# One level of Strassen in the up projection of an MLP: 256-token matmuls in place of 512

## What is computed

```
h2  = modulate(rms_norm(x, norm2_w), sh2, sc2)          # 512 x 2048
mlp = square(relu(h2 @ w_mlp1)) @ w_mlp2                # 2048 -> 8192 -> 2048
x   = x + g2 * mlp
out = rms_norm(x, final_norm_w)
```

## Time and profile before

| | |
|---|---|
| time, median of 3 runs | 2270.32 us (2270.09 to 2270.79) |
| the profiled execution | 2271.48 us, span 2269.7 us |
| TensorE busy | 2246.0 us |
| VectorE busy | 1581.5 us |
| ScalarE busy | 832.9 us |

### The profile page before, as it was taken

How to read it: one execution, slowest core, us unless ns; L and a number is a source line. 1 busy time by engine, 2 the same in 40 slices (tenths; PEclk the granted TensorE clock), 3 DMA queues, 4 the chain that set the end, 5 groups by cost and what they waited for, 6 DMA issues and landing times.

```text
span 2269.7 us, 27271 instructions
## 1 busy us (share of the span) xinstructions
PE 2246.0 (99%) x10096; PEld 1833.1 (81%) x10096; DVE 1581.5 (70%) x1898; ACT 832.9 (37%) x1106; POOL 119.1 (5%) x113
## 2 busy tenths in 40 slices
PE   8999999999999999999999999999999999999997
PEld 5588888888887888888888888888888888888886
DVE  8989888867666675634444444344789898989857
ACT  4333333344444422423323333333433333333343
POOL 0011111100101000000000000000000000000000
PEclk9999999999999999999999999999999999999999
DMA  9965777622222565434554455574775555555543
GB/s 400 420 247 203 260 258 255 251 86 81 78 79 75 203 260 194 147 113 176 175 197 173 166 199 179 172 281 171 265 275 206 222 203 191 216 222 203 221 163 135
DMA packets 110705, 455.24 MB, mean 201 GB/s; under 512 B 9009, under 2 KB 13617, under 8 KB 97073
## 3 DMA queue, kind: packets, MB, share of 16 engines
q1 hardware_dynamic: 101680, 394.49, 47.6%
q0 software_dynamic: 8672, 59.77, 7.1%
q10 hardware_dynamic: 290, 0.16, 0.0%
HBM read 390.42 MB, written 63.96 MB: 200 GB/s over the span
## 4 chain that ended last, share of the span: by engine, by line
PE 94%; issue 2%; DVE 2%; DMA 2%; ACT 0%; SPq 0%; POOL 0%; POOLq 0%; DVEq 0%; ACTq 0%
PE bank L733 20%; PE bank L734 20%; PE bank L737 20%; PE bank L1059 8%; PE bank L1050 8%; PE bank L1052 7%; PE bank L799 2%; PE bank L944 2%; PE bank L752 1%; DMA prob<-ada 1%; PE bank L1113 1%; PE bank L1115 1%; PE bank L1122 1%; PE bank L910 1%; DMA staged_kept<-staged_piece 0%
## 5 line engine op out<-in xcount | busy, mean ns | idle before, releaser
L733 PE MATMUL bank<-act_hi,w_hi 128*128 128x512 f32 x2016 | 790.3, 392 | 0.0
L734 PE MATMUL bank<-act_lo,w_hi 128*128 128x512 f32 x2016 | 784.9, 389 | 0.0
L737 PE MATMUL bank<-act_hi,w_lo 128*128 128x512 f32 x2016 | 498.1, 389 | 0.0
L1601 DVE TENSOR_TENSOR w_lo<-raw,w_hi 128x1024 fp32r<-128x1024 f32 x265 | 339.3, 1283 | 227.5 <-ACT w_hi L1201 226.0
L733 PEld LDWEIGHTS bank<-act_hi,w_hi 128*128 128x128 f32 x2016 | 378.6, 188 | 80.0 <-ACT w_hi L1201 1.5
L737 PEld LDWEIGHTS bank<-act_hi,w_lo 128*128 128x128 f32 x2016 | 378.4, 188 | 78.9 <-DVE w_lo L1601 0.5
L734 PEld LDWEIGHTS bank<-act_lo,w_hi 128*128 128x128 f32 x2016 | 378.6, 188 | 77.1
L1201 ACT ACTIVATE w_hi<-raw 128x1024 fp32r<-128x1024 f32 x265 | 279.5, 1055 | 284.4 <-PE bank L737 277.8
L2096 DVE TENSOR_TENSOR up_sb<-relu 128x512 f32<-128x512 f32 x64 | 44.1, 692 | 231.9 <-ACT relu L1463 231.9
L1050 PE MATMUL bank<-w_hi,form_sb 128*128 128x512 f32 x392 | 153.2, 391 | 1.8 <-issue 1.8
L1607 DVE CUSTOM_DVE_ANT_0 ada_sb<-ada_sb,silu_c 128x2048 f32<-128x2048 f32 x64 | 154.0, 2419 | 0.6 <-DMA ada_sb<-ada 0.6
(11 more groups left out here) (257 smaller groups left out, 2577.0 us busy)
## 6 DMA issues: line engine op xcount, KB each, us to landing
raw<-weights SPq DMA_DIRECT2D x272, 512.0 KB, 4.0
ada_sb<-ada SPq DMA_DIRECT2D x79, 1024.0 KB, 5.1
staged_kept<-staged POOLq DMA_DIRECT2D x51, 1024.0 KB, 4.7
form_sb<-staged_kept SPq DMA_DIRECT2D x49, 1024.0 KB, 4.8
quarter_b<-weights SPq DMA_DIRECT2D x18, 2048.0 KB, 11.2
quarter_a<-weights SPq DMA_DIRECT2D x17, 2048.0 KB, 7.9
xy<-x_t SPq DMA_DIRECT2D x16, 512.0 KB, 4.8
prob<-ada SPq DMA_DIRECT2D x8, 1024.0 KB, 10.1
```

What stands on the lines that cost most here:

```text
L733: pe.matmul(acc, stationary, hi, start=first, stop=False)
L734: pe.matmul(acc, stationary, lo, start=False, stop=False)
L737: mm = pe.matmul(acc, w_lo[:, w, i * P128:(i + 1) * P128], hi, start=False, stop=last)
L1601: nc.vector.tensor_tensor(w_lo[:, w], raw[:, r], w_hi[:, w].bitcast(F32), ALU.subtract).then_inc(lo_ready, 1)
```

## The change

Groups 1 to 7 of the up projection are computed by one level of Strassen as well. A unit is a pair of tiles: 256 columns of the weights, in four quadrants (two tiles by two halves of the 2048 rows), against h in four quadrants (two halves of the rows by two halves of the tokens). Seven forms of weights (made by VectorE per unit, in place in `raw`) meet seven forms of h (made once and kept in SBUF: quadrants of `act_hi` and `act_lo`, and `made5`, `made6`, `made3`).

- **TensorE:** `up_unit` replaces `up_tile`: seven steps of 24 matmuls, 256 tokens wide, into three half banks (`UP_CHAIN`), two sets of banks in turn. Some steps wait for ScalarE's copies of a bank (`copied`) or VectorE's closings (`closed`).
- **ScalarE:** per unit seven roundings (`up_hi`, four places), three copies of 128x256 out of PSUM (`copy_out`), and relu and square of the four quadrants (`square_out`); up to two staged forms.
- **VectorE:** per unit seven low halves (`up_lo`, two places), four sums of weights (`up_sum`), three closings (`close`) that add a copied chain to a bank into `up_sb`, and the staging work, now with sums made in place in `up_sb`.
- **Staging:** one place instead of two; the order of the forms is 1, 4, 5, 2, 7, 6, 3.
- **The opening:** during the last tiles of group 0 ScalarE fills `h_all` with the shifted h (`fill_h`, 16 of 128x512), VectorE makes four sums of 128x2048 in place (`sum_h`), and ScalarE and VectorE round forms 5, 3, 6, 7 (`h_hi`, `h_lo`). `normed` writes into `h_all` and no longer waits for a place.
- **Group 7** is written to DRAM unrounded (`pieces_kept`, 4 x 512 KB) and rounded in the last folded unit and at the start of its own product (`piece_high`, `piece_low`).
- **SP:** `load_unit` has four loads a unit; the first quarters and forms of the down projection are loaded during the last unit.

The core of the diff (PE, ScalarE, VectorE; the new `load_unit`, `sum_h`, `stage_lo` and the loads around the loops are told above):

```
+            def up_unit(w, q):
+                first = isinstance(w, int)
+                for k, form in enumerate(UP_FORMS):
+                    if k == 0 and first and w < 2:
+                        pe.wait_ge(relu_ready, BLOCKS)
+                    elif k == 0:
+                        pe.wait_ge(relu21, w - 1)
+                        pe.wait_ge(closed, 3 * w - 5)
+                    if k == 1 and not (first and w < 2):
+                        pe.wait_ge(closed, 3 * w - 3)
+                    if k == 2:
+                        pe.wait_ge(copied, 3 * w + 1)
+                    if k == 4:
+                        pe.wait_ge(copied, 3 * w + 3)
+                    if k == 6:
+                        pe.wait_ge(closed, 3 * w + 2)
...
+                    out = bank[3 * (q % 2) + UP_CHAIN[k]][:, 0:TOK // 2]
+                    high, low = up_hi_at(up_place(q, k)), w_lo[:, up_lo_place(q, k)]
+                    pe.wait_ge(hi_ready, UP_BASE + (N_FORMS * w + (k + 1)))
+                    for kk in range(BLOCKS):
+                        h_hi, h_lo = h_block(form, kk)
+                        cols = slice(kk * P128, (kk + 1) * P128)
+                        pe.matmul(out, high[:, cols], h_hi, start=k in UP_OPENS and kk == 0, stop=False, skip_group_check=True)
+                        pe.matmul(out, high[:, cols], h_lo, start=False, stop=False, skip_group_check=True)
+                    pe.wait_ge(lo_ready, UP_BASE + (N_FORMS * w + (k + 1)))
+                    for kk in range(BLOCKS):
...
+            for q in range(PAIRS):
+                up_unit(q, q)
+            with pe.Fori(1, FOLDED) as g:
+                for q in range(PAIRS):
+                    up_unit(4 * g + q, q)
...
+            def up_unit(g, q, par, w):            # ScalarE
+                up_hi(w, q, 0)
+                if q or not isinstance(g, int):
+                    before = (w - 1, (q - 1) % 4, par if q else 1 - par)
+                    square_out(*before, 1)
+                stage_hi(g, 1 - par, STAGES_A[q])
+                up_hi(w, q, 1)
+                if q or not isinstance(g, int):
+                    square_out(*before, 2)
+                    square_out(*before, 3)
+                copy_out(w, q, 0)
+                for k in (2, 3, 4):
+                    up_hi(w, q, k)
+                copy_out(w, q, 1)
+                up_hi(w, q, 5)
+                if q < 3:
+                    stage_hi(g, 1 - par, STAGES_B[q])
+                copy_out(w, q, 2)
+                up_hi(w, q, 6)
+                square_out(w, q, par, 0)
...
+            def up_unit(g, q, par, w):            # VectorE
+                if q or not isinstance(g, int):
+                    close(w - 1, (q - 1) % 4, par if q else 1 - par, 2)
+                up_lo(w, q, 0)
+                up_sum(w, q, 5)
+                stage_lo(g, 1 - par, STAGES_A[q])
+                up_lo(w, q, 1)
+                up_sum(w, q, 6)
+                up_sum(w, q, 7)
+                up_lo(w, q, 2)
+                up_sum(w, q, 4)
+                up_lo(w, q, 3)
+                up_lo(w, q, 4)
+                if q < 3:
+                    stage_lo(g, 1 - par, STAGES_B[q])
+                if q == 1:
+                    sum_stage(g, 1 - par, 7)
+                close(w, q, par, 0, g)
+                up_lo(w, q, 5)
+                close(w, q, par, 1)
+                up_lo(w, q, 6)
+                if q < 3:
+                    sum_stage(g, 1 - par, (5, 6, 3)[q])
...
             for t in range(4):                    # VectorE, the last tiles of group 0
-                for half in range(2):
+                for half in range(2 if t < 3 else 1):
                     rest_w(Count(C_MLP + 8 + 2 * t + half + 1))
+                if t == 3:
+                    h_lo(3)
+                    h_lo(6)
+                    up_lo(0, 0, 0)
+                    up_sum(0, 0, 5)
                 square_relu(4 + t, 0, 4 + t, t)
+                if t == 3:
+                    up_lo(0, 0, 1)
+                if t == 1:
+                    sum_h(0)
+                    sum_h(1)
+                elif t == 2:
+                    sum_h(2)
+                    sum_h(3)
+                    h_lo(5)
...
+                if t == 3:                        # ScalarE, the last tile of group 0
+                    up_hi(0, 0, 0)
                 take_u(4 + t, t, Count(C_MLP + 8 + 2 * t + 2), SPARE_UP if t == 0 else None)
```

More of the change, by code:

```diff
@@ L160 @@
 N_STEPS = STEPS * UNITS
[L161 to L167, removed]
+N_STAGED = N_FORMS * FOLDED
+C_UP = C_MLP + 2 * BLOCKS
+UP_FORMS = (1, 5, 6, 2, 7, 3, 4)
+UP_CHAIN = (0, 2, 0, 1, 0, 2, 0)
+UP_OPENS, UP_CLOSES = (0, 1, 3), (3, 5, 6)
+PAIRS = BLOCKS // 2
+UP_UNITS = PAIRS * FOLDED
+UP_STEPS = N_FORMS * UP_UNITS
+UP_SUMS = (5, 6, 7, 4)
+FILLED_AT = ((0, 1, 2, 3), (4, 5, 6, 7, 8, 9), (10, 11, 12), (13, 14, 15))
+LANDED_UP = (16 * (UP_UNITS // 2 + 1),) * 2 + (16 * (UP_UNITS + 1),) * 2
+STAGES_A, STAGES_B = (1, 5, 7, 3), (4, 2, 6)
 PAIR_OF = ((0, 1), (2, 2), (0, 1), (3, 3), (0, 1), (3, 3), (0, 1))
@@ L190, in form_stage, with up_lo_place, up_place @@
 def form_stage(g, form):
[L192 to L199, removed]
+    return N_FORMS * g + STAGED_FORMS.index(form)
+def up_lo_place(q, k):
+    return (7 * q + k + w_place(Count(C_UP - 2))) % 2
+def up_place(q, k):
+    return (7 * q + k) % 4
 def down_row(g, m):
     return PER_GROUP * g + (C_MLP + 2 * BLOCKS + m)
[L207 to L237, removed]
 def wd_slot(n):
@@ new lines, in stage_hi @@
+            def stage_hi(g, par, form):
+                stage = N_FORMS * g + STAGED_FORMS.index(form)
+                if not (isinstance(stage, int) and stage == 0):
+                    act.wait_ge(part_saved, 16 * stage)
+                else:
+                    act.wait_ge(usq_ready, BLOCKS)
+                if not isinstance(g, int):
+                    act.wait_ge(usq_ready, BLOCKS + (16 * g + (-8 if form == 1 else 0)))
+                if form in SUMMED_FORMS:
+                    act.wait_ge(sum_made, 4 + 4 * g + (SUMMED_FORMS.index(form) + 1))
+                nc.scalar.activation(staged[:, :, 0], up_block(par, form), ACT.Copy).then_inc(part_hi_ready, 1)
@@ L1541, in _ @@
+            square_out(*last, 3)
             for i in range(2, STEPS):
                 d_hi(0, 0, i)
-                if i in (6, 7):
-                    for stage, slot, kind, form in last_stages(i + 1):
-                        stage_hi(stage, slot, kind, form, FOLDED - 1, 0)
             for i in range(STEPS):
                 d_hi(1, 1, i)
-            with act.Fori(1, FOLDED) as g:
+            with act.Fori(1, FOLDED - 1) as g:
                 for j in range(2):
@@ L2295, in _ @@
                 for kp in range(4):
+                    if i == 0 and kp in (1, 2):
+                        piece_low(kp + 1)
                     last_lo(i, kp)
```

475 lines of the change are left out of this document (331 added, 144 removed).

## The result

The changed kernel takes 2234.69 us (median of 4 runs, 2234.05 to 2235.61) against 2270.43 of the kernel before (4 runs on the same chip, 2270.09 to 2270.79): ratio 0.9843, 95% interval 0.9826 to 0.9860. That is 35.7 us faster, where 40.5 was forecast.

The account below looks back on a forecast made before the run. TensorE, busy in 99% of the span, was taken to bound the kernel. Terms -44.8 + 7.8 - 4.0 + 0.5 = -40.5 us, off the median of 2270.32, gave 2229.8 us, range 2221 to 2256.

Parts of the forecast that it names:

- The matmuls: Up projection, groups 1 to 7: 28 pairs take 20.16 us each instead of 21.76, -44.8 us.
- The order inside a unit: Steady up units: VectorE's sums and ScalarE's roundings finish in time, form 6's with 0.9 us spare, so waits cost 0.
- the chain of sums: Steady up units: VectorE's low halves and sums alternate with ScalarE's roundings, six dependent steps, 0.9 us spare.
- its rival: Steady up units: the sums are not covered, each us lacking costs 28 us, 2258 at 1 us; chance 0.15.
- The single staging buffer: Up units: two staged blocks share one place; a turn takes 7.2 us, two are 14.4 of 20.16, so free.
- a sign that it is wrong: Up stage: ScalarE waiting for staged writes was listed among the observations that would show the prediction wrong; no size.
- The rival's threshold: Up units: writes over 7.6 us bound the unit, over 8.3 make the kernel slower; 2310 at 9 us; chance 0.07.
- The opening: Start of the folded up stage: late first start, waits in forms 5 to 7, second unit +0.5, clock 2: +7.8 us.
- The loop's code: Up stage: TensorE's bigger loop body does not stay, five returns wait 4.1 us each: 20 us, 2250; chance 0.07.
- none later: Up stage: TensorE waits in its first two units for rounded weights, a relu and a copy, and not afterwards.
- The opening of the down stage: First down unit: two fewer staged low halves and no last-write wait put VectorE 2.5 us earlier: -4.0 us.
- The pieces: Last group, written raw and rounded in the last folded unit: four roundings and four low halves, +0.5 us (0 to 2).

Follow-up runs that it names:

- The matmuls by themselves: A kernel of its own, TensorE alone, fp32r matmuls each with its own 128x128 load: 0.2267 us at 512 columns, 0.1199 at 256, 0.1113 at 128.
- shifted kernel: The changed kernel with group 0's staged blocks each moved on by one place, through the second place of unit 3: 2228.28 us.
- one operation more: The changed kernel with one extra VectorE sum over 128x1024 ahead of the first form's low half in each of 24 looped units: 2248.94 us.

## Why the prediction was right, and where its sum was off

It was right in direction and mechanism: 35.7 us faster for 40.5 forecast, 2234.7 inside the range of 2221 to 2256. The largest term was exact, and the small ones were off both ways: the opening +3.7 and the loop returns +1.7, the down unit -0.6, the pieces -0.5 and the end of the kernel -0.7, together 3.6 between -40.5 and the -36.9 of the profiled executions. That these partly cancel is luck. Point by point:

- **The matmuls, -44.8.** Exact: 0.120 us each, 2.88 a step, 20.16 a unit, clock 1.00. The matmuls by themselves show why 256 columns keep only 1.6 of 2.72 us a unit: 13 ns a matmul that do not shrink with the columns. The Trainium skill, "TensorE: Matmul & The Clock Gate" (LDWEIGHTS (loading the stationary operand)), gives the load 107 ns; the floor measured here, whatever sets it, is 111.
- **The order inside a unit, 0.9 us spare.** 0.64 measured. The reasoning on the chain of sums held, and so did the price of its rival: 1.13 us lacking in each of 24 looped units cost 27.3 us.
- **The single staging buffer, "free".** Half right. A turn was put at 7.2 us with the write's landing of 4.7. In the opening, with nothing else in its way, it took 1038.90 - 1030.56 = 8.3 us: the buffer is released 5.1 to 5.7 us behind the issue. In steady units that is hidden from TensorE, and so are 1.9 us more. But ScalarE does wait for staged writes there, which the prediction named as a sign that it is wrong; as a sign it was too strict, since such a wait costs nothing until an urgent rounding behind it is late. The rival's threshold, a write 2.9 us longer, lies between the 1.9 that cost nothing and the 3.4 that cost a unit 0.7 us; its mechanism is real, and in the steady units of the changed kernel it did not happen.
- **The opening, +7.8.** This is the term that was mis-sized: 11.5 us measured without the loop returns. First start 2.4 (measured 2.49 with the low half), form 5 1.1 (1.45), form 6 0.8 (0.86), form 7 1.0 (0.3). The step that failed is that staging was weighed over a steady unit only. In unit 0 the first block comes 10.7 us into the stage and the second is to follow 3.5 us later in ScalarE's queue, ahead of form 4's rounding: 2.48 us of hole and 1.6 of clock behind it, and in unit 1, put at 0.5, 2.14 for the same reason. The shifted kernel shows it: it gives back 6.1 us of these. The 1.6 us of clock are no cost of their own: what sets the end of unit 1 is when the buffer comes free the second time. With that write released 5.04 us behind its issue units 0 and 1 took 48.65 us with the clock loss (VectorE's loop written out), and with 5.06 us 48.66 without it (one operation more), since TensorE then waited longer in unit 1.
- **The loop's code.** Put at 20 us on TensorE with chance 0.07. TensorE's body of four units cost nothing at its returns (units 8, 16 and 24 take 20.16 us, and so do 12 and 20 once VectorE's loop is written out), as by the ISA Cache section of "Advanced Engine Details and Errata" of the Trainium skill it would. VectorE's return cost instead, 2.9 and 2.5 us of its time and 1.7 of TensorE's in two places, because 0.64 us of slack does not cover it. The rival was looked for on the wrong engine, and "none later", said of TensorE's waits, was wrong in these two places.
- **The opening of the down stage, -4.0.** -4.6 measured, all but 0.3 of the 4.9 us lost there before. Two low halves fewer are half of the cause, as shown; the other half went mostly with the clock.
- **The pieces, +0.5.** Nothing: the last folded unit takes 38.08 us like the others. The 0.7 us that the end of the kernel gained are the landing of the last writes, which varies between kernels.

## What to carry to other kernels

A buffer with one place has a turn, and it must be checked where the stage starts, not only where it runs: a start that is late by one turn queues several blocks close together, and each waits ahead of something urgent. Spread them over the places that are there; putting them off only moves the wait. And measure a chain's slack by adding one operation and then two: the first tells what is to spare, the second that nothing else hides, and an engine's idle share tells neither.

## What the hardware showed that I had not expected

- VectorE stood 2.3 to 3.0 us at each return of its loop of eight units, in all ten changed kernels that keep this loop. ScalarE stands at its returns as well, 2.91 and 3.05 us in the kernel with one operation more, where its row has nothing to wait for:

```profile
1261.07 1.06 ACT L1598 ACTIVATE w_hi<-raw 128x1024 fp32r<-128x1024 f32 x1 [2.91 <-issue]
```

  Only VectorE's reach TensorE: its holes go with VectorE's loop written out and stay with ScalarE's. From 1250 to 1450 us the first instruction queue moved 16 packets in the changed kernel and 10 with VectorE's loop written out, but also 10 with only ScalarE's written out, where VectorE's stall stays. What the stalls wait for is open.
- A fp32r matmul with its own 128x128 load takes 0.111 us at 192 and at 128 columns. At 64 columns the first forty also start 0.112 us apart, and then the granted clock falls to 0.50, the 1.2 GHz level, and they start 0.213 apart, though the page counts TensorE as busy all the time.
- The same hole does not always cost clock. The one of 2.3 us in unit 0 is followed by a step of 4.45 us for 2.88 in the changed kernel, at a mean granted clock of 0.61; in two other kernels with the same hole (one operation more; the first down unit) the step takes 2.95 us at 1.00. The windows, columns as in the earlier trace rows, of the changed kernel and of the one with two operations more in the first down unit:

```profile
1032.70:1037.10 4.40, 4.39 (x24) 4.40 (x25) 4.29 (x6) 2.26 (x5) 0.53 (x1) 0.61 0.72 228
...
1032.70:1035.60 2.90, 2.88 (x24) 2.90 (x25) 2.90 (x5) 2.27 (x5) 0.53 (x1) 1.00 0.55 209
```

  These two then waited longer in unit 1 (holes of 1.59 and 2.70 us for 0.78), as told above. Likewise the hole of 1.8 us in the first down unit had a step of 4.42 us behind it in the kernel before, and 2.84 in the run with two operations more. Holes of 0.3 to 0.7 us are followed by steps of 2.95 to 2.98.
